# A sparse-attention step with the values stationary, two heads in the halves of a PSUM bank, weights divided ahead of the transposes, and the result stored by features

## The reference

```
def dsa_attention(q, k, v, q_idx, k_idx, w_idx):      # 8 heads of 64
    topk = min(TOPK_MAX, S // 4)                      # 128
    def block(args):
        qb, qib, wb, start = args
        score = ...                                   # relu(q_idx . k_idx), weighted over 8 index heads
        score = jnp.where(admissible[None], score, -jnp.inf)
        top_val, top_idx = lax.top_k(score, topk)
        k_sel, v_sel = ...                            # the chosen keys and values
        logits = jnp.einsum('bqhd,bqkhd->bhqk', qb, k_sel) * (Dh ** -0.5)
        p = jax.nn.softmax(logits, axis=-1)
        return jnp.einsum('bhqk,bqkhd->bqhd', p, v_sel)
```

## Time and profile before

| | |
|---|---|
| median of 3 runs | 2794.98 us (2794.39 to 2796.49) |
| profiled execution | 2794.63 us, span 2793.3 us |
| mean granted TensorE clock | 0.994 |
| busy: PE, PEld | 97%, 78% |
| busy: DVE, ACT, POOL | 42%, 38%, 40% |
| chain that ended last | PE 93%, DVE 3%, ACT 2% |

### The profile page before, as it was taken

One profiled execution on the slowest core, in us unless ns is written; L12 is line 12 of the kernel. 1 busy time (PEld: TensorE's weight loads), 2 busy tenths in 40 slices (PEclk: granted clock), 3 DMA queues, 4 the chain that ended last, 5 costly groups with the idle time before them and its releaser, 6 DMA issues.

```text
span 2793.3 us, 36195 instructions
## 1 busy us (share of the span) xinstructions
PE 2718.8 (97%) x13753; PEld 2185.7 (78%) x13753; DVE 1175.1 (42%) x2435; ACT 1060.7 (38%) x2013; POOL 1127.5 (40%) x894
## 2 busy tenths in 40 slices
PE   7999999999989999999999999999999999999998
PEld 6887878898668877776788888887777678888887
DVE  3434343443445355433236424265533323642425
ACT  3333434353345334362333424234435233342422
POOL 4434343334332443322365444444332236544442
PEclk9999999999999999999999999999999999999999
DMA  5434343432321232223243333224222324333321
GB/s 179 136 106 124 97 117 95 121 129 83 106 77 61 85 117 77 75 87 109 91 158 107 106 98 98 91 81 131 82 72 88 106 90 159 107 106 99 98 91 60
DMA packets 214913, 286.40 MB, mean 103 GB/s; under 512 B 16846, under 2 KB 154546, under 8 KB 213972
## 3 DMA queue, kind: packets, MB, share of 16 engines
q1 hardware_dynamic: 214740, 284.08, 32.5%
HBM read 248.31 MB, written 18.94 MB: 96 GB/s over the span
## 4 chain that ended last, share of the span: by engine, by line
PE 93%; DVE 3%; ACT 2%; issue 1%; POOL 1%; DMA 0%; SPq 0%; DVEq 0%; ACTq 0%
PE banks L1636 37%; PE banks L1633 28%; PE banks L1629 13%; PE banks L1771 2%; PE banks L1654 2%; PE banks L1879 1%; PE banks L1753 1%; PE banks L1693 1%; PE banks L1669 1%; PE banks L1927 1%; PE banks L1738 1%; PE banks L1843 1%; PE banks L1857 1%; PE banks L1741 1%; DVE AF L2339 1%
## 5 line engine op out<-in xcount | busy, mean ns | idle before, releaser
L2922 POOL TENSOR_TENSOR WS<-WR,WS 128x512 fp32r<-128x512 f32 (+2 forms) x676 | 847.9, 1287 | 1105.2 <-ACT WS L1990 1105.2
L1636 PE MATMUL banks<-WS,UT 128*128 128x512 f32 (+1 forms) x3696 | 800.9, 366 | 6.2 <-DVE UT L2339 4.6
L1636 PEld LDWEIGHTS banks<-WS,UT 128*128 128x128 f32 x3696 | 605.2, 189 | 133.2 <-issue 32.2
L1633 PE MATMUL banks<-UT,WS 128*128 128x512 f32 (+1 forms) x2832 | 665.4, 393 | 0.7 <-ACT AR L2172 0.7
L1633 PEld LDWEIGHTS banks<-UT,WS 128*128 128x128 f32 (+1 forms) x2832 | 527.0, 188 | 125.1 <-issue 15.7
L1990 ACT ACTIVATE WS<-WR 128x1024 fp32r<-128x1024 f32 (+1 forms) x344 | 332.9, 1018 | 222.4 <-PE banks L1636 153.6
L1629 PE MATMUL banks<-UT,WS 128*128 128x512 f32 x1536 | 377.6, 399 | 0.0
L1629 PEld LDWEIGHTS banks<-UT,WS 128*128 128x128 f32 x1536 | 285.4, 190 | 65.9 <-issue 6.5
L1636 PE MATMUL banks<-WS,AT 128*128 128x512 f32 x1296 | 308.2, 396 | 0.0
L2920 POOL TENSOR_TENSOR WS<-WR,WS 128x512 fp32r<-128x512 f32 x128 | 177.1, 1415 | 275.9 <-ACT WS L1986 275.9
L1636 PEld LDWEIGHTS banks<-WS,AT 128*128 128x128 f32 x1296 | 242.6, 188 | 58.4 <-ACT WS L1990 0.7
(11 more groups left out here) (224 smaller groups left out, 2704.8 us busy)
## 6 DMA issues: line engine op xcount, KB each, us to landing
WR<-in_w_in SPq DMA_DIRECT2D x112, 512.0 KB, 3.4
WR<-in_w_up SPq DMA_DIRECT2D x88, 512.0 KB, 3.5
WR<-in_dil_w_in SPq DMA_DIRECT2D x64, 512.0 KB, 3.9
WR<-in_w_down SPq DMA_DIRECT2D x40, 512.0 KB, 3.7
WR<-in_diff_w_in SPq DMA_DIRECT2D x32, 512.0 KB, 3.7
WR<-in_dil_w_in SPq DMA_DIRECT2D x32, 256.0 KB, 3.8
AR<-AF SPq DMA_DIRECT2D x128, 64.0 KB, 2.0
AR<-AF SPq DMA_DIRECT2D x64, 128.0 KB, 2.4
```

Source lines behind the costliest of these rows:

```text
L1633: mm = pe.matmul(B[bank][0:c, :], w[part][:, kk, g * P:g * P + c], act[:, other, kk, :], start=start, stop=stop)
L1636: mm = pe.matmul(B[bank][:, off:off + n], act[:, other, before_k + kk, g * P:g * P + P], w[part][:, kk, :], start=start, stop=stop)
L2922: ge.tensor_tensor(slot(i, 1)[:, s], raw(i)[:, s], slot(i, 0)[:, s].bitcast(F32), ALU.subtract).then_inc(lo_p.sem, 1)
```

## The change

The result matmuls swap their operands: the values are stationary (64 columns) and the transposed weights move (128 columns). The two heads of a pair go to partitions 0 to 63 and 64 to 127 of one bank, in turn for each j. So the result has features on partitions, one out3 step serves two units (the one with odd n), and XA holds four chunks of 128 features x 512 tokens. The sums can no longer be divided out after the product, since they belong to tokens; VectorE scales the weights in place, in the turn3 step behind the reciprocal, and the transposes wait for that instead of for the exponential. A plain copy takes the place of the scaling after the product. The chunk steps need no transposes; they become "parts" steps, ScalarE's copy and VectorE's subtraction from XA. In the SP queue, load_h waits for the last low part instead of the last chunk transpose.

```diff
@@ -741,8 +741,9 @@
             def out_of(n):
-                self.step("out3", l, n)
-                yield
+                if n % 2:
+                    self.step("out3", l, n)
+                    yield
             yield from self.staged(len(units), [scores, turn, out_of])
@@ -814,7 +815,7 @@
             for c in range(4):
-                self.step("chunk", f"a{l}", c)
+                self.step("parts", f"a{l}", c)
                 yield
@@ -1695,16 +1700,11 @@
                     tag, c = a
-                    if tag in ("l1g", "l2g"):
-                        pe.wait_ge(timed.sem, timed.at[index[f"{tag}{c // 2}"], 1])
-                        src = X
-                    else:
-                        pe.wait_ge(out_copied.sem, out_copied.at["3", int(tag[1]), N3 - 1])
-                        src = XA
+                    pe.wait_ge(timed.sem, timed.at[index[f"{tag}{c // 2}"], 1])
                     k = bank6["chunk", tag, c]
...
                     for b in range(NB):
-                        mm = pe.transpose(B[k][:, b * P:b * P + P], src[:, b, c * P:c * P + P], IDN)
+                        mm = pe.transpose(B[k][:, b * P:b * P + P], X[:, b, c * P:c * P + P], IDN)
                     mm.then_inc(chunked.sem, 1)
@@ -1861,7 +1861,7 @@
                     b, e = sel_units[n][0], n % 2
-                    pe.wait_ge(exped.sem, exped.at["3", l, n])
+                    pe.wait_ge(weights_scaled.sem, weights_scaled.at["3", l, n])
                     k = bank6["turn", "3", l, n]
@@ -1871,13 +1871,14 @@
                     b, h = sel_units[n]
-                    e = n % 2
                     pe.wait_ge(pt_out.sem, pt_out.at["3", l, n])
...
                     for j in range(b + 1):
-                        mm = pe.matmul(B[ob][:, 0:64], arr(o_pt + 512 * e + j * P, P), av[:, j, h * 64:h * 64 + 64],
-                                       start=(j == 0), stop=(j == b))
+                        for e in range(2):
+                            o = (h - 1 + e) * 64
+                            mm = pe.matmul(B[ob][64 * e:64 * e + 64, 0:P], av[:, j, o:o + 64],
+                                           arr(o_pt + 512 * e + j * P, P), start=(j == 0), stop=(j == b))
                     mm.then_inc(summed.sem, 1)
@@ -2015,12 +2016,7 @@
                     src, d, _ = chunk_io(tag, c, B[bank6["chunk", tag, c]])
-                    if tag[0] == "a" and c == 0:
-                        l = int(tag[1])
-                        se.wait_ge(gated_o.sem, gated_o.at[l, NB - 1])
-                        for half in range(2):
-                            se.wait_ge(spilled[half].sem, spilled[half].at[index[f"m{l}gb3"], half])
-                    if tag in ("l1g", "l2g") and c == 0:
+                    if c == 0:
                         for name in "qk":
@@ -2030,6 +2026,16 @@
                         se.activation(d, src, ACT.Copy).then_inc(chunk_hi.sem, 1)
+
+                elif kind == "parts":
+                    tag, c = a
+                    l = int(tag[1])
+                    if c == 0:
+                        se.wait_ge(out_copied.sem, out_copied.at["3", l, N3 - 1])
+                        se.wait_ge(gated_o.sem, gated_o.at[l, NB - 1])
+                        for half in range(2):
+                            se.wait_ge(spilled[half].sem, spilled[half].at[index[f"m{l}gb3"], half])
+                    se.activation(EA[:, 0, c, :], XA[:, c, :], ACT.Copy).then_inc(chunk_hi.sem, 1)
                 elif kind == "pairs":
@@ -2206,7 +2212,7 @@
                         if n >= 2:
-                            se.wait_ge(recip.sem, recip.at["3", l, n + e - 2])
+                            se.wait_ge(weights_scaled.sem, weights_scaled.at["3", l, n + e - 2])
                         se.activation(v, v, ACT.Exp, bias=SM[:, MX + e:MX + e + 1], scale=-1.0,
@@ -2215,7 +2221,7 @@
                     if n >= 2:
-                        se.wait_ge(summed.sem, summed.at["3", l, n - 2])
+                        se.wait_ge(summed.sem, summed.at["3", l, n - 2 | 1])
                     se.activation(arr(o_pt + 512 * e, 512)[:, 0:w], B[bank6["turn", "3", l, n]][:, 0:w],
@@ -2386,6 +2392,11 @@
                         tt(d_lo, src, d_hi.bitcast(F32), ALU.subtract).then_inc(chunk_lo.sem, 1)
+
+                elif kind == "parts":
+                    tag, c = a
+                    ve.wait_ge(chunk_hi.sem, chunk_hi.at[tag, c])
+                    tt(EA[:, 1, c, :], XA[:, c, :], EA[:, 0, c, :].bitcast(F32), ALU.subtract).then_inc(chunk_lo.sem, 1)
                 elif kind == "rope":
@@ -2677,19 +2688,20 @@
                     e = n % 2
+                    v = arr(o_p + 512 * e, P * (sel_units[n][0] + 1))
                     ve.wait_ge(exped.sem, exped.at["3", l, n])
                     if n >= 2:
-                        ve.wait_ge(out_copied.sem, out_copied.at["3", l, n - 2])
+                        ve.wait_ge(weights_scaled.sem, weights_scaled.at["3", l, n - 2])
                     ve.reciprocal(SM[:, RZ + e:RZ + e + 1], SM[:, ZS + e:ZS + e + 1]).then_inc(recip.sem, 1)
+                    ve.wait_ge(recip.sem, recip.at["3", l, n])
+                    ve.tensor_scalar(v, v, SM[:, RZ + e:RZ + e + 1], None, ALU.mult).then_inc(weights_scaled.sem, 1)
                 elif kind == "out3":
...
                     b, h = sel_units[n]
-                    e = n % 2
                     ve.wait_ge(summed.sem, summed.at["3", l, n])
-                    ve.wait_ge(recip.sem, recip.at["3", l, n])
-                    ve.tensor_scalar(XA[:, b, h * 64:h * 64 + 64], B[bank6["out", "3", l, n]][:, 0:64],
-                                     SM[:, RZ + e:RZ + e + 1], None, ALU.mult).then_inc(out_copied.sem, 1)
+                    ve.tensor_copy(XA[:, h // 2, b * P:b * P + P],
+                                   B[bank6["out", "3", l, n]][:, 0:P]).then_inc(out_copied.sem, 1)
                 elif kind == "decay":
@@ -3103,7 +3115,7 @@
                     l, = a
-                    sy.wait_ge(chunked.sem, chunked.at[f"a{l}", 3])
+                    sy.wait_ge(chunk_lo.sem, chunk_lo.at[f"a{l}", 3])
                     sy.wait_ge(kdec.sem, kdec.at[l, NB - 1])
```

More of the change, by code:

```diff
@@ L1070, in build @@
         negated = tally("max_negated")
-        out_copied = tally("sums_scaled")
+        out_copied = tally("sums_copied")
+        weights_scaled = tally("weights_scaled")
         weighed = tally("weighed")
@@ L1194, in build @@
                 freed[k] = chunk_lo.plan(tuple(a))
+            elif kind == "parts":
+                chunk_hi.plan(tuple(a))
+                chunk_lo.plan(tuple(a))
             elif kind == "rope":
@@ L1232, in build @@
                     recip.plan(key)
+                    weights_scaled.plan(key)
                 freed[k] = pt_out.plan(key)
@@ L1508, in build @@
         o_y2, o_p, o_pt, o_r, o_sm = 12800, 13824, 14848, 15872, 3712
-        XA = arr(0, NB, 512)
+        XA = arr(0, 4, T)
         SEL = {1: arr(2048, 256), 2: arr(2304, 384), 3: arr(2688, 512)}
@@ L1555, in chunk_io @@
                         AT[:, 1, c, :].rearrange("p (l r) -> p r l", r=4))
-            d = EA if tag[0] == "a" else AT
-            return bank[:, :], d[:, 0, c, :], d[:, 1, c, :]
+            return bank[:, :], AT[:, 0, c, :], AT[:, 1, c, :]
         def width1(n):
```

## The result

The changed kernel takes 2864.34 us (median of 4 runs, 2860.95 to 2865.31) against 2794.7 us before (the 2794.98 ahead of the prediction is the median of three of these four runs): a ratio of 1.0244, interval 1.0228 to 1.026. Forecast was 2819, so the sign was right and the size was not: +70 instead of +25. The profiled execution has a span of 2859.6 us (before 2793.3, so +66.3), with a mean granted clock of 0.983 (before 0.994).

A forecast was written before the change was run, and what follows sets the result against it. TensorE, busy 97% of the span, was taken as the bound. The terms -8.4-3.5-8.1+36+2.8+3+3 gave +24.8 us on 2794.6, so 2819 us, with a range of 2784 to 2842.

The forecast's parts named there:

- Steps 1 to 3: TensorE's gains: result matmuls -8.4, chunk transposes gone -3.5, waits for the weights' copy gone -8.1; together -20 us.
- Step 3: Result matmuls of even units no longer wait for the copy of the transposed weights: -8.1 us.
- step 2: Chunk transposes go, -3.5 us; the copy and subtraction replacing them lie 13 us ahead of their reader and cost nothing.
- Step 4: Transposes of the attention weights wait for VectorE's reciprocal and scale: 18.0 a layer, +36 us, bounds 16 and 62.
- T27, T29 and T31: Weight transposes (turn3) of units 27, 29, 31, behind the decays: waits of 6.8 for the first two, 5.2 for the last.
- T0: Weight transposes (turn3) of unit 0, right behind its scores step: a new wait of 0.5 us in each layer.
- Step 5: Consequences: totals' wait +2.8, scales meeting GpSimd +3, lower TensorE clock +3 (each 0 to 8), earlier linear attention 0.
- T2, T10 and T28: Weight transposes (turn3) right behind the previous pair's result step, no projections between: waits of 1.9 us together a layer.
- VectorE in time: Rival: VectorE's scale slips into the time before the transposes, new waits below 20, 2777 to 2783 us; chance 0.16.
- halves without overlap: Rival: in the result matmuls the array's halves don't overlap at 128 columns, 2836 us; chance 0.10.
- waits about as large as the gains: Rival: transposes of units 27, 29, 31 fall elsewhere and cost little, time the same at 2795 us; chance 0.07.
- The waits are those of the old order: Rival: the transposes' waits for the scale total 62 us, as worked out for the old order, 2845 us; chance 0.07.

The follow-up runs named there:

- e6: Changed kernel without the division of the attention weights (transposes wait for the exponentials) and with the old number of attention steps: 2773.0 us, ratio 0.9924.
- e1: Changed kernel without reciprocal and scale, transposes waiting for the exponentials again, shorter attention order kept: 2804.2 us, ratio 1.0033 to the kernel before.
- e4: Changed kernel with reciprocal and scale planned on VectorE right behind the pair's maxima instead of at the transposes: 2808.8 us, ratio 1.0048.
- e9: Changed kernel with reciprocal and scale right behind the maxima, and 16 empty side-work turns a layer before the linear attention: 2780.2 us, ratio 0.9942.
- e5: Changed kernel with 16 throwaway 512-column matmuls a layer, keeping TensorE busy in its longest new stands: 2849.4 us, ratio 1.0197.
- e3: Changed kernel with the old number of attention steps, so the linear attention starts where it did before: 2856.7 us, ratio 1.0218.
- e8: Changed kernel with 16 empty side-work turns a layer between attention and linear attention, so what follows starts where it did before: 2835.6 us, ratio 1.0137.

## Why the prediction was wrong, step by step

The account of the changed kernel, in profiled spans: layout, transposes and copy's wait -22.8 (e6), T's wait +42.3 (44.5 less the 2.2 that it had), the tail's waits +15.2, lost clock +31.8. Sum +66.5, measured +66.3. With the result matmuls' wait of 3.6 where it occurs (e1, e4, e9) and the fillers in e5, the same account gives every other run to within some 6 us; it is furthest off for e3 (56.7, measured 62.9, of which 1.3 is one more wait of T) and e5 (50.1, measured 55.3), and what these have beyond it was not found.

- **Steps 1 to 3** (-20): right in sum, -22.8 by spans and -23.6 by medians, and in the one piece that I timed (1.24 against 1.21). Step 3 came with its 8.1 us of waits (none is left in e6); how the rest divides over steps 1 and 2 was not measured. The reader at 2303.15 us in step 2 belongs to m1pa, not m0pa; nothing hangs on it.
- **Step 4** (+36): right in kind and place, 6.3 too low for the 42.3 that are new. T27, T29 and T31 came as forecast. T0 of the first layer was to wait 0.5 more than its 0.93 before, and waits 2.39, because its scale of 128 columns took 1.23 instead of 0.2. These rows of the changed kernel's timeline show it beside a GpSimd group that ends at 1083.36, and the next scale of the same size behind that end, in 0.29:

```profile
1078.39 4.97 POOL L2934 TENSOR_TENSOR WS<-WR,WS 128x512 fp32r<-128x512 f32 x4 [3.10 <-ACT WS L1991]
...
1080.98 1.23 DVE L2697 TENSOR_SCALAR AR<-AR,SM 128x128 f32<-128x128 f32 x1
...
1083.69 0.29 DVE L2697 TENSOR_SCALAR AR<-AR,SM 128x128 f32<-128x128 f32 x1
```

  Step 5 had +3 for this meeting, so steps 4 and 5 together had 39 for 42.3. T2, T10 and T28, which had 1.9 together, wait 0.79, 1.46 and 1.72; the scales of T10 and T28 took 0.96 and 1.10 in the same way. The check by hand of the old order (62) was measured at 58.1 and 58.5.
- **Step 5 is the step that failed.** Its clock term was +3 with an upper bound of 8, and is 31.8. I took the row at 0.50 behind the two-column matmuls for the model of a clock fall and allowed one at T31, "perhaps those at T27 and T29". In the trace it fell behind stands of 2.4 and 2.7 as well, and behind totals and in the linear attention. The mechanism was named; its size was not worked out. By my measure a microsecond at 0.50 is half lost, 2.5 us in a window of 5; around T31 and totals alone the first layer has a loss of 2.50 (1265 to 1270) + 2.05 (1280 to 1285) + 2.50 (1285 to 1290) = 7 us, where the kernel before lost 1.7 behind totals.
- **Also in step 5**: 0 (-2 to +3) for the linear attention's earlier start, and +2.8 for totals. Measured are 10.2 (with the last transposes) and 5.0 of waits, and with the clock behind them the tail's start costs 29 (e8, e9). The reason given, fewer double steps that wait, did not hold: the states wait 12 times instead of 10. The tail's longest wait is on VectorE's queue: four products and a product of 1,024 columns stand ahead of the state that L1928 needs, and each of the four takes 1.3 us instead of 0.41 because it meets GpSimd (see e8).

```profile
1352.83 5.23 DVE L2770 TENSOR_SCALAR AR<-AR,SM 128x256 f32<-128x256 f32 x4 [1.12 <-POOL SM L2949]
...
1358.09 1.22 DVE L2345 TENSOR_TENSOR AR<-AR 128x1024 f32<-128x1024 f32 x1
1359.24 0.99 DVE L2739 SCALAR_TENSOR_TENSOR AR<-AR,SM,banks 128x256 f32<-128x256 f32 x2
...
1360.33 1.23 PE L1928 MATMUL banks<-AF 64*128 64x256 f32 x4 [2.93 <-DVE AR L2739]
```

- **The rivals**: VectorE in time, halves without overlap, and waits about as large as the gains are all refuted. "The waits are those of the old order" is what e3 is; it took 2856.7, not 2845, with 40.0 us of lost clock where step 5 had 3 more than the 16.8 of before.
- **The prediction's last sentence** said that it would fail first on the places of T27, T29 and T31. Those were right.

Left open: between the profiled executions the tail's start makes 22.5 us (changed kernel and e8) and 27.8 us (e4 and e9), of which waits and lost clock explain 15.2 + 6.0 and 15.2 + 11.4. The waits are the same in both pairs; why the lost clock is not was not found. Which of totals, linear attention and last transposes costs most was not separated, and that GpSimd's meeting with the products causes the linear attention's waits is read from the rows of eleven kernels, not from a run that moves GpSimd alone.

## What to carry to other kernels

When a wait is put on the busiest engine, add to its length what the engine does slowly behind it: here 42.3 us of new waits for the scale brought some 26 us of lost clock (e8 against the kernel before). A step that must end before TensorE reads belongs in the other engine's queue right behind its own input, not at its reader: the same division costs 5 to 7 us there, and 60 at the transposes in the shorter order, 84 in the old one. And a change that shortens an interleaved side stream moves all that follows in it; hold the followers in place, or work out their waits as carefully as those of the changed step, GpSimd's instructions beside them included.

## What the runs showed that I had not expected

The granted clock fell behind stands of only 2.4 to 3.1 us: windows of 5 us at 0.68 to 0.87 behind stands of 3.10, 3.08, 2.72 and 2.39 in the first layer, against 1.00 in the same places when fillers took most of the stand (e5). But the length of a stand alone does not decide it. The second layer has the same stand of 2.39 at T0, and there the clock stayed up; in e8's second layer it fell behind a stand of 1.75, while 1.72 in the first left it at 1.00. Changed kernel, T0 of the first and of the second layer with the windows behind them, then e8:

```profile
1085.00:1090.00 5.00, 5.00 (x23) 3.81 (x21) 0.00 (x0) 0.77 (x2) 0.00 (x0) 0.86 0.25 92
```
```profile
2023.46 0.33 PE L1868 MATMUL banks<-CT,AR 128*128 128x128 f32 x1 [2.39 <-DVE AR L2697]
2025.00:2030.00 5.00, 4.82 (x24) 3.55 (x22) 0.32 (x2) 0.77 (x2) 0.00 (x0) 1.00 0.34 109
```
```profile
2165.00:2170.00 5.00, 3.42 (x10) 2.42 (x10) 1.49 (x4) 1.16 (x2) 5.00 (x4) 0.68 0.36 100
```

So in these runs the clock lost behind one short stand was partly luck. Useless matmuls in front of a wait made the kernel 0.5% faster.

And the time of a scale says little of its width; by shape, at the same 16 of each:

```profile
L2697 DVE TENSOR_SCALAR AR<-AR,SM 128x128 f32<-128x128 f32 x16 | 10.8, 678 | 0.6
L2697 DVE TENSOR_SCALAR AR<-AR,SM 128x512 f32<-128x512 f32 x16 | 9.0, 563 | 0.6
```

What decides is whether an instruction of GpSimd is running when the scale starts. Of the changed kernel's 64 scales, 24 start beside one and take 0.70 to 1.26 us; each of them ends 0.08 to 0.29 us after that GpSimd instruction. The other 40 take 0.29 to 0.49. The 24 cost 15.6 us more than the others of their widths. In this trace, then, a scale that comes second waits for GpSimd's instruction of some 1.3 us to end.
